# Router fed by the transposed residual with the norm applied to its logits, and a pieced first load with later row turns in the modulation stage

## The reference, cut to what matters

```python
sh1, sc1, gt1, sh2, sc2, gt2 = split(silu(c) @ w_mod + b_mod, 6)     # the modulation, 6 x 1024 columns
h   = rms_norm(x, g_norm1) * (1 + sc1) + sh1                         # feeds the token mixers
x1  = x + gt1 * (y @ w_out)                                          # the residual after the mixers
h2  = rms_norm(x1, g_norm2) * (1 + sc2) + sh2
p_grp    = softmax(h2 @ w_grp + b_grp)                               # router: 4 group logits
e_logits = h2 @ w_rexp + b_rexp                                      # and 16 expert logits
# top-1 group, top-2 experts in it, SwiGLU experts on h2, gated and added to x1, final RMSNorm
```

## Time and profile before

| | |
|---|---|
| three runs | 2410.28, 2411.46, 2413.93 us, median 2411.46 |
| the profiled execution | 2409.13 us, span 2407.4 us, mean granted TensorE clock 0.945 |
| front | 0 to 131.8 us of the span |
| mix_out | 1383 to 1747.3 us |
| experts and combine | from 1747.8 us |

### The profile page before, as it was taken

How to read it: one execution, slowest core, us unless ns; L and a number is a source line. 1 busy time by engine, 2 the same in 40 slices (tenths; PEclk the granted TensorE clock), 3 DMA queues, 4 the chain that set the end, 5 groups by cost and what they waited for, 6 DMA issues and landing times. The chain is left out here.

```text
span 2407.4 us, 26509 instructions
## 1 busy us (share of the span) xinstructions
PE 2160.3 (90%) x10126; PEld 1744.5 (72%) x10126; DVE 1406.8 (58%) x1681; ACT 1026.3 (43%) x1348; POOL 836.8 (35%) x615
## 2 busy tenths in 40 slices
PE   6979999998798995899999769999969999998992
PEld 1258887887687884788888657777758778887882
DVE  0629552110333322789988445445378899998993
ACT  1422211110243444455655344433245676666763
POOL 5300000000355653466766412220113444443541
PEclk9989999999899996799999979999869999999996
DMA  7733415211754765244355386574269965469425
GB/s 281 254 76 97 120 53 197 83 48 44 253 170 145 188 166 179 84 133 129 116 138 137 79 259 197 168 235 140 88 267 368 362 214 168 114 194 338 133 53 166
DMA packets 263322, 399.26 MB, mean 166 GB/s; under 512 B 27350, under 2 KB 187222, under 8 KB 256412
## 3 DMA queue, kind: packets, MB, share of 16 engines
q1 hardware_dynamic: 233500, 244.42, 32.0%
q0 software_dynamic: 27968, 147.89, 19.6%
q10 hardware_dynamic: 1728, 5.25, 0.6%
HBM read 402.21 MB, written 88.67 MB: 204 GB/s over the span
## 5 line engine op out<-in xcount | busy, mean ns | idle before, releaser
L2747 DVE TENSOR_TENSOR ex_w_lo<-ex_raw,ex_w_hi 128x2048 fp32r<-128x2048 f32 x186 | 416.2, 2286 | 39.8 <-ACT ex_w_hi L2609 39.8
L2609 ACT ACTIVATE ex_w_hi<-ex_raw 128x2048 fp32r<-128x2048 f32 x182 | 337.4, 1909 | 176.1 <-DMA ex_raw<-in_w_up_dram,rt_w_rows 90.9
L834 POOL DMA_DIRECT2D vals<-rows_out x40 | 21.8, 545 | 438.5 <-ACT rows_out L826 438.5
L2479 POOL DMA_INDIRECT ex_raw<-in_w_up_dram,rt_w_rows x60 | 77.8, 1296 | 139.9 <-DVE ex_w_lo L2747 134.1
L2479 POOL DMA_INDIRECT ex_raw<-in_w_down_dram,rt_w_rows x30 | 52.5, 1751 | 185.7 <-DVE ex_w_lo L2747 153.6
L919 PE MATMUL gl_u_ps<-half_hi,gl_u_w_hi 128*128 128x512 f32 x256 | 108.8, 425 | 3.2 <-ACT gl_u_exp L937 3.2
L919 PE MATMUL ml_u_ps<-half_hi,ml_u_w_hi 128*128 128x512 f32 x256 | 106.1, 414 | 6.1 <-ACT ml_u_exp L937 6.1
L826 ACT ACTIVATE rows_out<-rows_ps 128x512 f32<-128x512 f32 x40 | 23.9, 599 | 198.2 <-PE rows_ps L793 198.2
L2538 PE MATMUL ex_g_ps<-ex_w_hi,ex_x_hi 128*128 128x512 f32 x248 | 103.0, 415 | 6.0 <-DVE ex_x_lo L2752 5.8
L2264 PE MATMUL mo_ps<-mo_branch_hi,mo_w_hi 128*128 128x512 f32 x256 | 105.3, 411 | 2.5 <-POOL mo_branch_lo L2088 1.3
L2538 PE MATMUL ex_y_ps<-ex_w_hi,ex_hidden_hi 128*128 128x512 f32 x248 | 99.9, 403 | 7.1 <-DVE ex_w_lo L2747 7.1
(11 more groups left out here) (424 smaller groups left out, 6079.4 us busy)
## 6 DMA issues: line engine op xcount, KB each, us to landing
fr_w<-in_w_mod_dram SPq DMA_DIRECT2D x12, 2048.0 KB, 10.0
ml_u_w<-in_w_in_dram SPq DMA_DIRECT2D x32, 512.0 KB, 5.1
gl_u_w<-in_w_in_dram SPq DMA_DIRECT2D x32, 512.0 KB, 5.2
vals<-rows_out POOLq DMA_DIRECT2D x40, 256.0 KB, 2.3
ml_v<-vals SPq DMA_DIRECT2D x20, 512.0 KB, 4.2
gl_v<-vals SPq DMA_DIRECT2D x20, 512.0 KB, 3.5
qk_w<-in_w_in_dram SPq DMA_DIRECT2D x16, 512.0 KB, 4.7
ml_rows<-scan_rows SPq DMA_DIRECT2D x16, 512.0 KB, 6.0
```

What stands on the lines that cost most here:

```text
L2479: pool.indirect_dma_start(out=raw[:, q, :], out_offset=None, in_=sources[q], in_offset=bass.IndirectOffsetOnAxis(ap=w_rows[:, q, b:b + 1], ...
L2609: act.activation(hi[:, q, h], raw[:, q, h], ACT.Copy).then_inc(hi_done[q], 1)
L2747: dve.tensor_tensor(lo[:, q, at], raw[:, q, at], hi[:, q, at].bitcast(F32), ALU.subtract)\
```

## The change

Three edits. **In front**, the weights of blocks 0 and 1 are loaded as four pieces of two k each, each piece with a semaphore of its own for which TensorE waits before that piece's matmuls. And out(n) of blocks 0 to 2, 9 and 10 is issued behind rows(n+1) instead of rows(n).

**In mix_out**, the router takes the transposed x1 instead of the transposed h2. Its weights are scaled once by g_norm2*(1+sc2) (`router_weights`, on VectorE in step 8), the constant sh2 @ W is made once (`router_base`, on TensorE behind unit 9 and on VectorE in step 11), and the logits are multiplied by the token's r and get the constant added (`keep_logits`). For that SP loads three more columns of 1024 numbers, behind the existing one. h2 is still made and stored, for the experts. In the first half `turn_h`, `router` and `tile_turned` come one step earlier, and `load_x(i)` waits for `turn_h(i-2)`, because x1's slot is now read by the transposes. In the second half each half row (4 transposes) is turned right behind the following unit's matmuls, and the routers of tiles 4 and 5 are put before and into the last unit; the last tile's `shift` moves from GpSimd to VectorE.

```diff
@@ front, SP
+                for q in range(4) if n < IN_PIECES else ():      # IN_PIECES = 2
+                    k = slice(q * KD // 4, (q + 1) * KD // 4)
+                    sp.dma_start(wt[:, n, k, :], wsrc[:, k, n * COLS:(n + 1) * COLS]).then_inc(first_loaded[n][q], 16)
+                if n >= IN_PIECES:
+                    load(n)
@@ front, TensorE
                 for k in range(KD):
+                    if n < IN_PIECES and k % (KD // 4) == 0:
+                        pe.wait_ge(first_loaded[n][k // (KD // 4)], 16)
...
                 rows(n)
+                if n - 1 >= 0 and not beside_tokens(n - 1) and n - 1 != COLUMN_BLOCKS - 1:
+                    out(n - 1)
                 for t in tiles_before(n):
                     turn(t)
-                out(n)
+                if beside_tokens(n) or n in (COLUMN_BLOCKS - 1, NB - 1):   # beside_tokens: 4 <= n < 9
+                    out(n)
@@ mix_out, SP
                 if i >= 2:
                     sp.wait_ge(h2_part, i - 1)
+                    sp.wait_ge(h_turned, i - 1)
...
+                for n, src in enumerate((m.mod_rows[0:1, D:2 * D], m.mod_rows[0:1, 2 * D:3 * D], w["g_norm2"][0:1, :])):
+                    sp.dma_start(mod2[:, n, :], src.rearrange("a (k p) -> p (a k)", p=P)).then_inc(mod2_loaded, 16)
@@ mix_out, ScalarE
+            def keep_half(n):
+                c, t = n // TH, n % TH
+                act.wait_ge(half_turned, n + 1)
...
+                act.activation(xt_late[:, 4 * c:4 * c + 4, t * P:(t + 1) * P],
+                               ps[:, half_bank(n), :].rearrange("p (k n) -> p k n", n=P), ACT.Copy).then_inc(half_kept, 1)
...
-                if 0 <= at - 4 < TH:
-                    tile_turned(first + at - 4)
+                if 0 <= at - 3 < TH:
+                    tile_turned(first + at - 3)
...
+                if 0 <= u - LAST - 2 < TH:
+                    keep_half(u - LAST - 2)
             tile_norm(TH)
+            keep_half(TH)
             tile_norm(TH + 1)
-            tile_turned(TH)
+            keep_half(TH + 1)
             tile_norm(TH + 2)
+            keep_half(TH + 2)
             tile_norm(TH + 3)
-            for i in range(TH + 1, NL):
-                tile_turned(i)
+            keep_half(TH + 3)
@@ mix_out, GpSimd
-            for i in range(NL):
+            for i in range(NL - 1):
                 shift(i)
@@ mix_out, VectorE
+                dve.tensor_tensor(some, ps[:, 7, 0:TH * RL].rearrange("p (t n) -> p t n", n=RL),
+                                  st2[:, first:first + TH, 2:3].to_broadcast([P, TH, RL]), ALU.mult).then_inc(logits, 1)
+                dve.wait_ge(logits, 2 * (first // TH) + 1)
+                dve.tensor_tensor(some, some, base[:, :].rearrange("p (a n) -> p a n", a=1).to_broadcast([P, TH, RL]),
+                                  ALU.add).then_inc(logits, 1)
...
+            dve.tensor_tensor(last, last, spread[:, 0, :], ALU.add).then_inc(last_shifted, 1)
@@ mix_out, TensorE
             def turn_h(i):
-                pe.wait_ge(h2_done, i + 1)
+                pe.wait_ge(x1_done, i + 1)
...
-                                        h2[:, i % 2, k * P:(k + 1) * P], m.ident[:, :])
+                                        x1[:, i % 2, k * P:(k + 1) * P], m.ident[:, :])
...
+            def turn_half(n):
+                c, t = n // TH, n % TH
+                pe.wait_ge(row_half, n + 1)
...
+                for k in range(4):
+                    at = (4 * c + k) * P
+                    last = pe.transpose(ps[:, half_bank(n), k * P:(k + 1) * P], hin[:, t, at:at + P], m.ident[:, :])
+                last.then_inc(half_turned, 1)
...
+                if 0 <= at - 2 < TH:
+                    turn_h(first + at - 2)
                 if 0 <= at - 3 < TH:
-                    turn_h(first + at - 3)
-                if 0 <= at - 4 < TH:
-                    router(first + at - 4)
+                    router(first + at - 3)
...
-            for u in range(LAST, NU):
+            for u in range(LAST, NU - 1):
                 out_rows(u)
-                if u == NU - 2:
-                    turn_h(TH)
-            router(TH)
-            for i in range(TH + 1, NL):
-                turn_h(i)
-                router(i)
+                if u > LAST:
+                    turn_half(u - LAST - 1)
+            router_late(0, 0)
+            router_late(0, 1)
+
+            def second_late():
+                turn_half(TH + 2)
+                router_late(1, 0)
+                router_late(1, 1)
+            out_rows(NU - 1, [second_late])
+            router_late(2, 0)
+            router_late(2, 1)
+            router_late(3, 0)
+            turn_half(TH + 3)
+            router_late(3, 1)
```

More of the change, by code:

```diff
@@ L201, in front @@
                 "out_moved", "a1_ready", "stat", "xn_ready", "turned", "scaled", "split_hi", "split_lo"))
+        IN_PIECES = 2
+        first_loaded = [[sem(f"fr_first_loaded{n}{q}") for q in range(4)] for n in range(IN_PIECES)]
+        loads_before = lambda n: n // SLOTS - (1 if n % SLOTS < IN_PIECES else 0)
         block = ctx.enter_context(nc.Block())
@@ L1806, in mix_out @@
         gt1 = sb("mo_gt1", [P, KD])
+        mod2 = sb("mo_mod2", [P, 3, KD])
+        wr_shift = sb("mo_w_router_shift", [P, KD, GROUPS + EXPERTS])
+        base = sb("mo_router_base", [P, GROUPS + EXPERTS])
         spread = sb("mo_spread", [P, 2, D])
@@ L1932, in store_h2 @@
             def store_h2(i):
-                sp.wait_ge(h2_done, i + 1)
+                if i == NL - 1:
+                    sp.wait_ge(last_shifted, 1)
+                else:
+                    sp.wait_ge(h2_done, i + 1)
                 sp.dma_start(m.h2[i * P:(i + 1) * P, :], h2[:, i % 2, :]).then_inc(h2_stored[i % 2], 16)
@@ L2199, in tile_steps @@
                 if at == TH + 4:
+                    dve.wait_ge(base_kept, 1)
                     keep_logits(first)
@@ L2224, in _ @@
                     scale_in(u // KD + 1, u % KD - 3)
+                if u == KD:
+                    router_weights()
+                if u == KD + 3:
+                    router_base()
                 tile_steps(u - AFTER_O, 0)
@@ L2227, in _ @@
             normed(NL - 1)
+            dve.wait_ge(h2_part, NL)
+            last = h2[:, (NL - 1) % 2, :]
+            dve.tensor_tensor(last, last, spread[:, 0, :], ALU.add).then_inc(last_shifted, 1)
             keep_logits(TH)
-            dve.wait_ge(logits, 2)
+            dve.wait_ge(logits, 4)
         @block.tensor
@@ L2267, in unit, with out_rows @@
                 last.then_inc(made, 1)
-            def out_rows(u):
+            def out_rows(u, between=()):
                 c, t = out_piece(u)
@@ L2280, in out_rows @@
                         pe.wait_ge(yl_done, KD + k + 1)
+                    if k == KD // 2:
+                        for work in between:
+                            work()
                     pe.matmul(out, y_hi[:, k, at], br_hi[:, c, k, :], start=(k == 0), stop=False)
@@ L2305, in router, with router_base, router_late @@
                 pe.wait_ge(h_t, i + 1)
-                if i == TH:
-                    pe.wait_ge(logits, 1)
-                elif i == 0:
-                    pe.wait_ge(wr_loaded, 32)
+                if i == 0:
+                    pe.wait_ge(wr_scaled, 3)
+                    pe.wait_ge(base_kept, 1)
                 for k in range(KD):
-                    last = pe.matmul(ps[:, 7, i % TH * RL:(i % TH + 1) * RL], h2t[:, k, :], wr[:, k, :],
+                    last = pe.matmul(ps[:, 7, i * RL:(i + 1) * RL], h2t[:, k, :], wr[:, k, :],
                                      start=(k == 0), stop=(k == KD - 1))
                 last.then_inc(routed, 1)
+            def router_base():
+                pe.wait_ge(wr_scaled, 1)
+                pe.matmul(ps[:, 7, 0:KD * RL], m.ones[:, :], wr_shift[:, :, :].rearrange("p k n -> p (k n)"),
+                          start=True, stop=True).then_inc(base_made, 1)
+            def turn_half(n):
+                c, t = n // TH, n % TH
+                pe.wait_ge(row_half, n + 1)
+                if n == 0:
+                    pe.wait_ge(h_t, TH)
+                elif n >= 2:
+                    pe.wait_ge(half_kept, n - 1)
+                for k in range(4):
+                    at = (4 * c + k) * P
+                    last = pe.transpose(ps[:, half_bank(n), k * P:(k + 1) * P], hin[:, t, at:at + P], m.ident[:, :])
+                last.then_inc(half_turned, 1)
+            def router_late(t, c):
+                pe.wait_ge(half_kept, TH * c + t + 1)
+                if t == 0:
+                    pe.wait_ge(logits, 1)
+                for k in range(4 * c, 4 * c + 4):
+                    last = pe.matmul(ps[:, 7, t * RL:(t + 1) * RL], xt_late[:, k, t * P:(t + 1) * P], wr[:, k, :],
+                                     start=(k == 0), stop=(k == KD - 1))
+                if c:
+                    last.then_inc(routed, 1)
             def tile_steps(at, first):
```

36 lines of the change are left out of this document (29 added, 7 removed).

## The result

The changed kernel takes 2394.11 us (median of 4 runs, 2391.87 to 2396.84), the kernel before beside it 2410.87 (2406.29 to 2413.93, 4 runs): ratio 0.9935, 95% interval 0.9921 to 0.995. The profiled execution has a span of 2392.3 us against 2407.4.

The account below looks back on a forecast made before the run. Read stage by stage: load landings and row waits bound front, TensorE's serial routers and turns mix_out's end. Terms -3.0 - 3.7 + 0.7 + 0.3 + 0.2 - 6.9 = -12.4 us gave 2399.0, range 2393 to 2409.

Parts of the forecast that it names:

- front: Front stage: loading in pieces gains 3.0 us and moving out(n) behind the next block's rows 3.7, together 6.7.
- start of mix_out to unit 24: Start of mix_out: three column loads cost 0.7 us of stall on unit 3, the constant and scaling 0.3.
- units 24 to 32: First half of mix_out: turns and routers one step earlier, with one fall of the clock, end 0.2 us later.
- tail: End of mix_out: the store of h2's last tile becomes the end; gain 6.9 us, bounds 4.5 and 8.
- the move: Front: out(n) issued behind the next block's rows removes TensorE's waits for the row; gain 3.7 us, bounds 2.8 to 4.6.
- I take the cold start's 1.5 us off: Front: TensorE idles some 3.7 us before block 2, so a slow clock cuts the pieces' gain from 4.5 to 3.0 us.
- Rival 2: Front: six pieces pay about 1.8 us each in series, block 2 lands 10.8 later; 2409.8 us, no change; chance 0.07.
- Rival 1: Start of mix_out: each column load occupies the queue for 7.0 us, unit 3 stalls 20.2; 2418.6 us; chance 0.05.
- 1.5 - 0.8 = 0.7 us of stall on unit 3: Start of mix_out: three column loads at 0.5 us each, less 0.8 us of cover before unit 3's first product.
- 2.0 + 2.5: First half of mix_out: TensorE idles 2.0 us at turn_h(1) and 2.5 at turn_h(2), waiting for ScalarE's copies.
- Rival 3: First half of mix_out: load_x behind the turns brings a second clock fall and longer stalls; 2402 to 2405 us; chance 0.14.
- Rival 4: End of mix_out: another wait takes TensorE's place and the tail gives nothing; 2405.9 us; chance 0.04, with others.

Follow-up runs that it names:

- the three more: Changed kernel with three more column loads of the same sources, into a tile nothing reads, behind the first three: 2396.35 us, ratio 0.994.
- the last kernel: Changed kernel with ScalarE's copy of the turned tile first, three blocks in pieces and the column loads on GpSimd's queue: 2386.55 us, ratio 0.9882.

## Why the prediction was right

My terms, and what the traces gave: the changed kernel's first profile, then the spread over the profiles in which the part in question is unchanged (for the second row, those with the three column loads in place and not doubled), each against the one profile of the kernel before:

| step | forecast | measured |
|---|---|---|
| front | -6.7 | -7.6; -7.6 and -7.9 with block 2 at the low clock, -9.4 to -9.5 without (119.12 to 119.29, five profiles) |
| start of mix_out to unit 24 | +1.0 | +3.6; +1.5 to +4.7 over seven profiles |
| units 24 to 32 | +0.2 | -4.0; +0.3 to -4.0 over nine profiles, mean -1.7 |
| tail | -6.9 | -6.7; -6.3 to -7.4 over the eleven profiles with the shift unmoved |

**Front.** The mechanism was right in what carried the gain: block 2's landing as the next wait (30.6, not 31.7), the 0.93 gaps gone, 3.6 for the move (3.7). The first product at 11.90 (12 forecast) is luck: the first quarter landed at 10.2, 1.8 us earlier than I had it, and TensorE was held by ScalarE's conditioning columns, a wait that my step doesn't have. It cost nothing, since block 2's landing was still the limit. In the first profile the mis-sized term is that landing, 1.1 us earlier than forecast (36.23 - 30.58 = 5.65 less 1.7 for the slow clock is 4.0, where I had 4.5 less 1.5 = 3.0). "I take the cold start's 1.5 us off" held there (1.7) and failed more often than not: the slow clock behind that wait came in two profiles of seven with this front, and without it the front gains 9.4. Rival 2, a fixed cost for each piece in series, is refuted: two blocks of pieces bring block 2 in at 30.6, three have it running at 28.0. The rate while the pieces arrive, 12 to 16 us, is 396 GB/s, against 389 with whole loads. The Trainium skill, "DMA: Bandwidth & Descriptors", section "Bandwidth", asks for at least 1 MiB a transfer, by a table of loads issued from GpSimd; for these quarters of 512 KB, queued together by SyncE, the trace shows no loss.

**Column loads.** Rival 1 with 7.0 each is refuted; my 0.5 us each is the low end for the first three (the issue of unit 3's weights shifts by 2.6 us in the first profile and by 1.4 to 2.8 over the seven, not by 1.5), and lies inside what the three more cost (0.1 to 0.6 each). What failed is the step "1.5 - 0.8 = 0.7 us of stall on unit 3": the cover was smaller than that shift, and I priced no clock behind a stall. From leaving unit 1 to leaving unit 5 it took 23.3 us before, 24.8 with the wait of 1.06 us and 27.1 with 2.12 and the low clock behind it; the longer wait cost 1.7 us more than itself. Of the first profile's +3.6, another 1.4 is the slow unit 1, a fall of the clock that has nothing to do with these loads and that my sum doesn't have. The constant's product took its place without a wait that the profile shows; its share in what is left between 188.6 and 189.6 to 190.0 wasn't separated.

**First half.** The step "2.0 + 2.5" was wrong in its second part: VectorE could start on the x tile 3.8 us after its issue, not 5.5, so ScalarE's copy was in time and turn_h(2) never waited. One wait of 1.59 stood where 2.0 was forecast, and the wait at turn_x(3), "as before" in my step (1.64), was anything from 0.66 to 2.05. The price of the clock's fall was left at 3.1 for one fall; over nine profiles the stretch varied by 4.2 us with the same wait of 1.59, and the wait ahead of it by 1.4, so most of that is the clock's. Without the wait it is 59.6, so the fall and the wait together cost 3.4 to 7.6. Rival 3, a second fall, didn't come.

**Tail.** Right in what ends it: the last store, by its landing in both profiles and by moving the shift. Right in size by two errors that cancel: unit 47 ends 92.8 us after unit 32 is left, where the forecast's 1730.7 means 91.8, and the store took 2.6 us where I had 3.5. Rival 4 is refuted. How much of the 6.7 belongs to the transposed residual, to the turning by half rows and to the order of the routers was not tried apart.

The errors had both signs. In the first profile they add up to 2.3 us of further gain: 0.9 in front and 4.2 in units 24 to 32 more, 2.6 at mix_out's start and 0.2 in the tail less. The rest of the 4.9 us between the forecast and the median is the scatter of medians of a few runs; the changed kernel's own were 2394.1 and 2395.8. What the kernel gains beyond that scatter is therefore front and tail. The two middle rows together give -0.4 in one profile of the very kernel and +2.7 in the other, and by the means of their spreads (+3.4 and -1.7) the middle loses some 1.7 us. That the forecast of the total came within 4.9 us owes something to these errors meeting.

## What to carry to other kernels

Price a new wait on TensorE twice: the idle time, and the slow clock that can follow it. Look for what stands ahead of the copy or the load that TensorE waits for; exchanging two operations on ScalarE's queue and moving three tiny loads behind the ones on the path gave, with one block more in pieces, 8.5 us between profiles, more than half as much again as the whole change (15.1). A profile's gain in a stretch with such a wait in it needs a second profile of the same kernel before it is believed. And when a start comes where it was forecast, look at what released it: here it was not the load.

## What the runs showed of the hardware

In mix_out, TensorE's single idle times of 0.64 us (the kernel with ScalarE's order changed), 1.06 (unit 3) and 1.39 (the last kernel, in the place of that 0.64) left the granted clock at 1.00. The wait of 1.59 us, with another of 0.66 to 2.05 us some 2 us ahead of it, was followed by a fall in each of the nine profiles that have it. In front, the wait for block 2 was followed by a fall where it was 0.90, 1.90 and 1.92 us, and by none where it was 1.53, 2.26, 2.41 (twice) and 2.92. At the end of mix_out's unit 0, a wait of 1.24 us for GpSimd was followed by a fall in the three profiles where another of 0.72, 1.10 or 1.19 us stood some 2 us ahead of it (unit 1 took 7.0 to 7.1 us), and by none in the seven where that one was 0.53 us or less (5.6). Unit 12's wait was 3.06 to 3.29 us in all thirteen profiles; the unit took 8.3 to 9.6 us in eleven of them and 6.9 in two, behind waits of 3.06 and 3.23. The length of the idle time alone doesn't tell, then; what else does was not tried.

VectorE's small operation on the logits took 1.58 us beside GpSimd's shift, and 0.24 without it. And SyncE was held for 5 to 7 us in the issue of two small loads (4 to 64 KB) behind the four mo_in tiles, whatever these small loads were; the ones behind them took 0.6 each. What holds it there, no view shows.
